# The first scores of attention made between the last jobs of the projection

## What is computed

```python
h = rmsnorm(x, g_pre_mix[l])
proj = jnp.einsum('bsd,dc->bsc', h, w_in[l])
fq, fk, fv, f_logit, dq, dk, dv = jnp.split(proj, split_idx, axis=-1)
...
# forgetting attention, one block of 128 queries (c: running sum of log sigmoid(f_logit))
s = jnp.einsum('bqhd,bkhd->bhqk', q_i, k).astype(jnp.float32) * scale
s = s + c_i[..., :, None] - c[..., None, :]
s = jnp.where(mask, s, -jnp.inf)
p = jax.nn.softmax(s, axis=-1)
o = jnp.einsum('bhqk,bkhd->bqhd', p.astype(v.dtype), v)
```

## Time and profile before

| | us |
|---|---|
| median of 3 runs | 2805.8 |
| the runs | 2801.6, 2805.8, 2806.15 |
| the profiled execution, whole | 2801.12 |
| its span from first to last instruction | 2799.4 |
| TensorE busy in the span | 2725.3 |
| end of the projection's matmuls | about 567 |
| attention's start on TensorE | 569.5 |

### The profile page before, as it was taken

One profiled execution on the slowest core, in us unless ns is written; L12 is line 12 of the kernel. 1 busy time (PEld: TensorE's weight loads), 2 busy tenths in 40 slices (PEclk: granted clock), 3 DMA queues, 4 the chain that ended last, 5 costly groups with the idle time before them and its releaser, 6 DMA issues.

```text
span 2799.4 us, 36795 instructions
## 1 busy us (share of the span) xinstructions
PE 2725.3 (97%) x13362; PEld 2253.3 (80%) x13362; DVE 1756.6 (63%) x2495; ACT 1344.5 (48%) x2413; POOL 629.6 (22%) x558
## 2 busy tenths in 40 slices
PE   8999999989999999999999999999999999999998
PEld 6888888878787787877788788888888888888887
DVE  6211111169889889899846778887777544435567
ACT  5121111168788788788523545464444433322233
POOL 5220021026746646556411100000000000000012
PEclk9999999999999999999999999999999999999999
DMA  5443343464434514414346755565345555546566
GB/s 190 131 153 101 104 136 113 144 148 98 105 83 97 128 52 118 123 41 120 106 128 217 260 204 199 186 237 201 134 149 196 180 186 209 185 159 224 203 219 240
DMA packets 287660, 434.49 MB, mean 155 GB/s; under 512 B 19648, under 2 KB 134592, under 8 KB 287488
## 3 DMA queue, kind: packets, MB, share of 16 engines
q1 hardware_dynamic: 241664, 368.41, 42.4%
q10 hardware_dynamic: 45056, 63.05, 6.2%
q0 software_dynamic: 768, 0.79, 0.1%
HBM read 280.27 MB, written 151.91 MB: 154 GB/s over the span
## 4 chain that ended last, share of the span: by engine, by line
PE 68%; DVE 5%; ACT 4%; issue 3%; POOL 0%; ACTq 0%; POOLq 0%; DVEq 0%
PE ml_ps L2845 7%; PE ml_ps L2843 7%; PE ml_ps L2844 7%; PE ml_ps L2813 7%; PE ml_ps L2815 7%; PE ml_ps L2816 7%; PE at_ps_t L1486 5%; PE at_ps_s L1462 4%; PE at_ps_s L1468 3%; PE mo_acc L1801 2%; PE mo_acc L1803 2%; PE mo_acc L1802 2%; PE at_ps_o L1501 2%; PE at_ps_o L1502 2%; ACT at_probs L1313 2%
## 5 line engine op out<-in xcount | busy, mean ns | idle before, releaser
L1361 DVE TENSOR_REDUCE at_nmax<-at_ps_s 128x1 f32<-128x1024 f32 (+7 forms) x384 | 346.6, 906 | 37.0 <-PE at_ps_s L1468 34.8
L2813 PE MATMUL ml_ps<-ml_h_hiM,ml_w_hi 128*128 128x512 f32 x896 | 349.1, 390 | 1.0 <-DVE ml_t L2635 0.9
L2816 PE MATMUL ml_ps<-ml_h_hiM,ml_w_lo 128*128 128x512 f32 x896 | 348.7, 389 | 0.0
L2815 PE MATMUL ml_ps<-ml_h_loM,ml_w_hi 128*128 128x512 f32 x896 | 348.7, 389 | 0.0
L2845 PE MATMUL ml_ps<-ml_b_hi,ml_a_lo 128*128 128x512 f32 x896 | 348.6, 389 | 0.0
L2844 PE MATMUL ml_ps<-ml_b_lo,ml_a_hi 128*128 128x512 f32 x896 | 348.6, 389 | 0.0
L2843 PE MATMUL ml_ps<-ml_b_hi,ml_a_hi 128*128 128x512 f32 x896 | 348.6, 389 | 0.0
L598 DVE SCALAR_TENSOR_TENSOR pj_out_sb<-pj_acc,pj_out_sb 128x512 fp32r<-128x512 f32 x96 | 66.4, 691 | 424.1 <-ACT pj_out_sb L534 424.1
L1370 DVE TENSOR_TENSOR at_p_lo<-at_ps_t,at_p_hi 128x512 fp32r<-128x512 f32 x480 | 280.0, 604 | 35.8 <-ACT at_p_hi L1331 32.7
L1331 ACT ACTIVATE at_p_hi<-at_ps_t 128x512 fp32r<-128x512 f32 x480 | 248.5, 533 | 87.6 <-PE at_ps_t L1486 48.0
L2490 POOL TENSOR_SCALAR ml_ss<-ml_ss 128x1 f32<-128x1 f32 x16 | 17.6, 1099 | 1183.7 <-ACT ml_junk L2583 1183.4
(11 more groups left out here) (264 smaller groups left out, 5981.3 us busy)
## 6 DMA issues: line engine op xcount, KB each, us to landing
ml_a_raw<-ua SPq DMA_DIRECT2D x112, 512.0 KB, 3.9
qk<-pj_out_sb ACTq DMA_DIRECT2D x64, 512.0 KB, 2.8
ml_w_raw<-in_w_up_dram SPq DMA_DIRECT2D x64, 512.0 KB, 5.1
ua<-ml_t SPq DMA_DIRECT2D x128, 256.0 KB, 2.6
ml_b_raw<-in_w_down_dram SPq DMA_DIRECT2D x56, 512.0 KB, 4.9
at_q<-qk SPq DMA_DIRECT2D x96, 256.0 KB
at_k<-qk SPq DMA_DIRECT2D x96, 256.0 KB
ua<-ml_x SPq DMA_DIRECT2D x96, 256.0 KB, 2.6
```

Of the source, the lines that this page charges most:

```text
L1361: dve.tensor_reduce(nmax[:, par, sc.a, s, sc.part:sc.part + 1], ps_s[:, sc.g % 2, 0:sc.width], AX.X, ALU.max, negate=True).then_inc(maxed, 1)
L2813: pe.matmul(to, hi, h_hi[m][:, k, :], start=begins and k == 0, stop=False, skip_group_check=not begins)
L2815: pe.matmul(to, hi, h_lo[m][:, k, :], start=False, stop=False, skip_group_check=not begins)
L2816: last = pe.matmul(to, lo, h_hi[m][:, k, :], start=False, stop=k == 3, skip_group_check=not begins)
```

## The change

Twelve score tiles, those of blocks 0, 1 and 2 (`OPENING`), are made in the projection, between the matmuls of the value jobs 10 to 14. Each value job has two places: one after half of its chunks, one after its last matmul. `opening_slots` gives the tiles to the ten places in order; a tile of 256 shares its place with the tile of 128 behind it. VectorE makes the maxima and ScalarE the exponentials in the same places of their own programs. For this the tiles and PSUM buffers of attention and the semaphores `scored`, `maxed` and `exped` are laid out in `Lasting`, ahead of both stages; the probability ring begins at column 70; the value jobs 8 to 15 use the four upper banks only, since the scores take the lower four. The score matmuls themselves go into a function `score_tile`, which both stages call. The planner treats the steps of these tiles as done, at no cost. The rest of `attend` is the same code with less indentation.

```diff
@@ projection_jobs
-        bank = m % 4 if m < 12 else m % 8
+        bank = m % 4 if m < 12 else m % 8 if (what, n) != ("val", 1) or rb < RT // 2 else 4 + m % 4
@@ Lasting
+        self.scored, self.maxed, self.exped = (r.sem(name) for name in ("scored", "maxed", "exped"))
+        with ExitStack() as fourth:
+            r = Room(nc, fourth, "at")
+            r.start_at(128)
+            self.o_sb = r.sb("o_sb", [P, ORING, 512])
...
+            self.ps_s = r.ps("ps_s", [P, 2, 1024])
+            self.ps_t = r.ps("ps_t", [P, TRING, 512])
+            self.ps_o = r.ps("ps_o", [P, 512])
@@ project
+    def tiles_at(job, half):
+
+        if (job.what, job.n) != ("val", DIFF):
+            return []
+        return slots.get(2 * job.rb + half - FIRST_SLOT, [])
+
+    lower_banks = max(m for m, job in enumerate(jobs) if job.bank < 4)
@@ project, ScalarE
+            def open_exp(sc):
+                at, par = places[sc.b, sc.a] + sc.lo, sc.b % SETS
+                act.wait_ge(maxed, sc.g + 1)
+                act.activation(keep.probs[:, at:at + sc.width], keep.ps_s[:, sc.g % 2, 0:sc.width], ACT.Exp,
+                               bias=keep.nmax[:, par, sc.a, 0, 0:1], accum_out=keep.rsum[:, par, sc.a, 0, 0:1])\
+                   .then_inc(exped, 1)
...
+                for sc in tiles_at(job, 0):
+                    open_exp(sc)
...
+                for sc in tiles_at(job, 1):
+                    open_exp(sc)
@@ project, VectorE
+            def open_max(sc):
+                dve.wait_ge(scored, sc.g + 1)
+                dve.tensor_reduce(keep.nmax[:, sc.b % SETS, sc.a, 0, 0:1], keep.ps_s[:, sc.g % 2, 0:sc.width], AX.X,
+                                  ALU.max, negate=True).then_inc(maxed, 1)
@@ project, TensorE
+            def open_score(sc):
+                b = blocks[sc.b]
+                if sc.g == 0:
+                    pe.wait_ge(evacuated, lower_banks + 1)
+                if sc.g >= 2:
+                    pe.wait_ge(exped, sc.g - 1)
+                pe.wait_ge(keep.q_loaded[b.qb], 64)
+                for p in pieces_of(sc):
+                    pe.wait_ge(keep.k_loaded[p], 64)
+                score_tile(pe, keep, blocks, sc).then_inc(scored, 1)
...
                     for k in range(KT):
+                        if k == KT // 2:
+                            for sc in tiles_at(job, 0):
+                                open_score(sc)
...
                     last.then_inc(multiplied, 1)
+                    for sc in tiles_at(job, 1):
+                        open_score(sc)
@@ constants, planner
+FIRST_COLUMN = 70
+OPENING = 3
+FIRST_SLOT = 20
...
-    places, former, owner, at = {}, {}, [None] * (PROB_COLUMNS // P), 0
+    places, former, owner, at = {}, {}, [None] * (PROB_COLUMNS // P), FIRST_COLUMN
...
+        if arg in self.done:
+            holds, result, urgency, after = 0.0, 0.0, -10.0, ()
+def opening_slots(scores):
+
+    tiles = opening_tiles(scores)
+    slots, n = defaultdict(list), 0
+    for sc in tiles:
+        slots[n].append(sc)
+        if sc.width > 256 or sc.a == 0:
+            n += 1
+    return slots
@@ attend
+    opening = opening_tiles(scores)
+    steps = [step for step in attention_steps(blocks, scores, turns) if step[1] not in opening]
```

882 lines of the change are left out of this document (445 added, 437 removed).

## The result

| | before | after |
|---|---|---|
| median | 2805.9 us (6 runs, 2801.6 to 2807.3) | 2817.6 us (6 runs, 2816.1 to 2821.2) |
| the profiled execution, whole | 2801.1 us | 2816.7 us |
| its span | 2799.4 us | 2815.0 us |

The change makes the kernel slower: the ratio is 1.005, with a 95% interval of 1.0039 to 1.0060. Forecast were 2805.0 us and a range that ended at 2811.0. The prediction was wrong.

What follows compares the result with a forecast made beforehand. TensorE, busy 2725.3 of 2799.4 us, was the bound, gaining only where it waits or runs at low clock; 6.9 + 0.8 + 12.5 = 20.2 against 21.0 gave -0.8 us, hence a 2805.0 us median, range 2799.5 to 2811.

Steps and rivals of the forecast that it cites:

- Tiles in the projection: Value jobs 10 to 14: twelve score tiles with masks add 6.9 us (6.0 to 7.3) to TensorE's path.
- the term for the masks: Score tiles in the projection: twelve 128-column masks cost up to 0.7 us more than the pace gives.
- Tile 0: First place, middle of value job 10: waiting for query and key tile 0 costs +0.8 us (0 to 2.0).
- Maxima and exponentials, banks: In the projection: VectorE's and ScalarE's added work and four banks instead of eight cost nothing.
- Barrier: Between projection and attention: TensorE's 2.52 us without work stay.
- Block 3's first score: Behind the barrier: it starts 12.5 us after TensorE's start there, bounds 10.5 and 15.
- first copy: Behind the barrier: ScalarE's copy into p_hi waits for the projection's stores, +2.3 to +2.9 us.
- first value product: Behind the barrier: starts after the transposes of tiles 4 to 6, about +5.8 us, not at +4.9.
- The wait for p_lo: Behind the barrier: TensorE waits for the subtraction's result from about +1 to +3.6 us.
- The sum at equal work: Up to block 3's first score: 20.2 us after the change against 21.0 before, -0.8 us.
- The rest of attention: Behind block 3's first score: order kept but for some transposed tiles pulled ahead, priced at 0 (-2 to +2 us).
- The clock stays low: Rival behind the barrier: half pace through block 3's first two scores, +4.3 to +6.5 us; 0.16 together with late tiles.

Runs made afterwards that it cites:

- e1: The changed kernel (after) with the ten score places one value job later; 2813.9 us, ratio 1.0041 to before.
- e4: The changed kernel with no tile moved and the probability ring at column 0, layout and four upper banks kept; 2804.2 us, ratio 1.0002 to before.
- e9: The changed kernel with places one value job later and the ring at its old columns from block 3 on; 2809.8 us, ratio 1.0017 to before.
- e17: e9 with the planner giving no cost to loads the projection has already made (keys 0 and 1, query tiles 0 and 1); 2804.6 us, ratio 1.0001 to before.
- e18: e9 with keys 2 and 3 and query tile 2 loaded in the projection, planner unchanged; 2808.4 us, ratio 1.0015 to before.

## Why the prediction was wrong, step by step

- **Tiles in the projection, +6.9 us.** Right: 7.2 us in e1. One reading in it was loose: nine transposes took 1.78 us from start to start (576.15 to 577.93) and not 2.12, which makes the term for the masks 0.2 us smaller.
- **Tile 0, +0.8 us.** Mis-sized. The wait was 1.87 us, just under the bound of 2.0. The keys' last piece was issued at 532.70 and landed at 539.2 us, 6.5 us later and not the 5.2 of the values in the earlier trace rows. The 1.65 MB that the queue had moved by 537 us were no sign that the first 1.6 MB were in: by then over 2.3 MB had been issued, the second query tile among them. The estimate from the fixed cost of about 2.0 us in the Trainium skill ("DMA: Bandwidth & Descriptors", "Anatomy of one DMA") was a wait of 1.9 us. The number agrees; the row doesn't separate a receipt from queueing behind other transfers, so it doesn't confirm the reason, and the page tells of GpSimd's path. What I had left out altogether is the clock behind a wait in a dense stretch: 1.7 us. I had weighed the low clock only behind the barrier.
- **Maxima and exponentials, banks: nothing.** Right: no place but the first waits, and e4, which has the four upper banks, is at 1.0002.
- **Barrier, +2.5 us.** Right: 2.37.
- **Block 3's first score at +12.5 us.** Nearly right as the sum of a chain (13.55). Its parts: first copy at +3.2 (2.3 forecast), first value product at +6.9 (5.8), low clock up to there and beyond. The wait for p_lo that was forecast from +1 to +3.6 came, a microsecond later (+2.2 to +4.6).
- **The sum at equal work, -0.8 us.** Measured +3.5. The difference of 4.3 is 3.2 in the projection (0.3 tiles, 1.1 wait, 1.8 clock and rest) and 1.1 behind the barrier. All of this lies within the range that was given.
- **The rest of attention at nothing, -2 to +2.** This step failed, and it is three quarters of the error: 15.6 - 3.5 = 12.1 us in the traces. Four places of the ring are 3.4 of them, one fall of the clock without a cause in the code is 1.6 (block 21), and some 7 lie in blocks 3 to 7, where the order was at fault (4.5 to 6.1 us from e9 to e17, by ratio and by median). I took block 3's first score for the end of the disturbance because the order behind it looked like that of before. I had not asked why the order ahead of it put that score behind eight value products. A TensorE that had just waited 2.4 us, with scores ready to be made, was in my own forecast (the wait for p_lo), and the chain that I priced was one that the plan had made, not one that the data needed. e17 shows the other order: with a plan that knows the loads, block 3's first score starts at +1.4 and the loss is gone. The ring's start, which I had seen as one changed place per pair of units, cost 0.85 us each time and not nothing.
- **Rivals.** "The clock stays low" came closest: its mark, a clock not back by +9, is what the trace shows (0.50 until +9.5, back at full from +10.5). But its mechanism, block 3's first scores at half pace, did not come (the clock was 1.00 there), and the measured 11.7 us at block 8 lie far above its bound of 6.5. I gave it too little, and without the cause.

Between the profiled executions the loss is 15.6 us, between the medians 11.8. The choice of execution explains the 3.8 us between: the profiled one of before was among its fastest (2801.1 us, 4.7 below the median), that of after 0.9 below its own. The parts, each as a difference of distances to before in medians: ring 4.6, first place 2.0 (3.5 in the trace), plan 6.1 (e9 to e17; 3.8 between e18 and e17). They sum to 12.7, or 10.4, against 11.8. By the ratios, the ring is 3.9, the first place 2.5 and the plan 4.5 us, 10.9 of 14.0. Each part is uncertain by 2 to 4 us and they were measured on different bases, so the three causes are shown one by one, and up to 3 us of the loss may have another.

## What to carry to other kernels

When a step is taken out of a stage whose order comes from a planner, take out what feeds it too: a load that is already made but still planned holds back everything that depends on it. Behind a barrier, work that needs nothing new is the cover for the first transfers and conversions; whoever moves it ahead of the barrier has to name what covers them now. A new wait in a dense stretch of TensorE costs its own length and, in some cases (behind the 1.87 us at the first place, the 1.65 us at 610 and the 1.91 us at 620 us of after), some 1.7 us of clock behind it.
